# A two-layer diffusion backbone: the order of weight sums, block loads and drains in the Strassen part of layer 0's MLP

## The reference, cut to what matters

```
def _sq_relu_mlp(h, w1, w2):          # h: (768 tokens, 1024), w1: (1024, 4096), w2: (4096, 1024)
    return jnp.square(jax.nn.relu(h @ w1)) @ w2
...
x = _layernorm(DN_ALPHA * x + g2 * _sq_relu_mlp(x * (1.0 + s2) + sh2, ffn_w1[i], ffn_w2[i]), ln2_g[i], ln2_b[i])
```

## Time and profile before

| | us |
|---|---|
| median of 3 runs (lowest, highest) | 1959.92 (1959.57, 1962.16) |
| the profiled execution | 1959.92 |
| its span, first to last instruction | 1958.1 |
| PE busy | 1945.9 (99%) |
| DVE, ACT, POOL busy | 1312.5 (67%), 642.7 (33%), 385.9 (20%) |

### The profile page before, as it was taken

One profiled execution on the slowest core, in us unless ns is written; L12 is line 12 of the kernel. 1 busy time (PEld: TensorE's weight loads), 2 busy tenths in 40 slices (PEclk: granted clock), 3 DMA queues, 4 the chain that ended last, 5 costly groups with the idle time before them and its releaser, 6 DMA issues.

```text
span 1958.1 us, 25025 instructions
## 1 busy us (share of the span) xinstructions
PE 1945.9 (99%) x9525; PEld 1668.2 (85%) x9525; DVE 1312.5 (67%) x1892; ACT 642.7 (33%) x894; POOL 385.9 (20%) x360
## 2 busy tenths in 40 slices
PE   9999999999999999999999999999999999999998
PEld 6889889889889988899888888888888888888887
DVE  4756678688778776777865553644554477777778
ACT  3423222234323322232533223313323344344443
POOL 0300311322222222112350110020020026100004
PEclk9999999999999999999999999999999999999999
DMA  9623334335898998898322132121222125976656
GB/s 338 249 65 76 108 123 130 94 118 151 203 249 209 217 230 221 238 231 206 114 70 65 54 102 65 54 92 54 75 65 81 58 83 173 241 217 188 181 142 149
DMA packets 110833, 282.95 MB, mean 144 GB/s; under 512 B 16256, under 2 KB 29184, under 8 KB 110592
## 3 DMA queue, kind: packets, MB, share of 16 engines
q1 hardware_dynamic: 84496, 219.34, 33.8%
q0 software_dynamic: 24400, 58.21, 17.0%
q10 hardware_dynamic: 1824, 3.85, 0.6%
HBM read 234.67 MB, written 2.12 MB: 121 GB/s over the span
## 4 chain that ended last, share of the span: by engine, by line
PE 92%; DVE 2%; POOL 2%; DMA 2%; issue 2%; ACT 1%; SPq 0%; POOLq 0%; DVEq 0%; ACTq 0%
PE bank L999 17%; PE bank L1001 17%; PE bank L1000 17%; PE bank L1038 7%; PE bank L1039 7%; PE bank L1037 7%; PE bank L1400 3%; PE bank L1402 3%; PE bank L1403 3%; PE bank L1604 2%; PE bank L1602 2%; PE bank L1605 2%; PE bank L1307 1%; PE bank L1356 1%; PE bank L1219 1%
## 5 line engine op out<-in xcount | busy, mean ns | idle before, releaser
L2099 DVE TENSOR_TENSOR w_lo<-raw,w_hi 128x1024 fp32r<-128x1024 f32 x132 | 171.4, 1298 | 244.5 <-ACT w_hi L1628 244.4
L1628 ACT ACTIVATE w_hi<-raw 128x1024 fp32r<-128x1024 f32 x132 | 139.4, 1056 | 371.4 <-PE bank L1039 198.6
L1037 PE MATMUL bank<-w_hi,hT_hi 128*128 128x512 f32 x592 | 230.8, 390 | 0.0
L1038 PE MATMUL bank<-w_lo,hT_hi 128*128 128x512 f32 x592 | 230.5, 389 | 0.0
L1039 PE MATMUL bank<-w_hi,hT_lo 128*128 128x512 f32 x592 | 230.5, 389 | 0.0
L999 PE MATMUL bank<-w_hi,act_hi 128*128 128x512 f32 x504 | 198.4, 394 | 0.0
L1001 PE MATMUL bank<-w_hi,act_lo 128*128 128x512 f32 x504 | 196.6, 390 | 0.0
L1000 PE MATMUL bank<-w_lo,act_hi 128*128 128x512 f32 x504 | 196.5, 390 | 0.0
L999 PE MATMUL bank<-hT_hi,w_hi 128*128 128x384 f32 (+2 forms) x544 | 192.4, 354 | 0.0
L1001 PE MATMUL bank<-hT_hi,w_lo 128*128 128x384 f32 (+2 forms) x544 | 191.0, 351 | 0.0
L1000 PE MATMUL bank<-hT_lo,w_hi 128*128 128x384 f32 (+2 forms) x544 | 191.0, 351 | 0.0
(11 more groups left out here) (390 smaller groups left out, 4337.0 us busy)
## 6 DMA issues: line engine op xcount, KB each, us to landing
raw<-w_units_d SPq DMA_DIRECT2D x242, 512.0 KB, 3.8
mod<-mod_units_d SPq DMA_DIRECT2D x64, 384.0 KB, 4.4
wsum<-w_units_d SPq DMA_DIRECT2D x45, 512.0 KB, 4.5
wsum<-w_units_d POOLq DMA_DIRECT2D x26, 512.0 KB, 7.7
wsum<-wsum POOLq DMA_DIRECT2D x19, 512.0 KB, 6.7
bv<-mod_units_d SPq DMA_DIRECT2D x16, 512.0 KB, 3.6
mod<-mod_units_d SPq DMA_DIRECT2D x14, 512.0 KB, 7.9
res_lat<-rbuf POOLq DMA_DIRECT2D x28, 256.0 KB, 5.1
```

The costliest lines, as they stand in the source:

```text
L1037: nc.tensor.matmul(bank[t][:, :], hT_hi[:, kc, tt], hi[:, c], start=kc == 0, stop=False)
L1038: nc.tensor.matmul(bank[t][:, :], hT_hi[:, kc, tt], lo[:, c], start=False, stop=False)
L1628: nc.scalar.activation(halves_of(phase, k, i)[0], raw[:, s, :], ACT.Copy).then_inc(hi_done, 1)
L2099: tt(lo, raw[:, s, :], f32(hi), ALU.subtract).then_inc(lo_done, 1)
```

## The change

It moves T4's first term, its slot, and the order of several items. No arithmetic is added or removed except the source of T4's two terms. In the steady pieces:

- T4 is built in slot 1 (T1's): SP loads B21 into it a second time after T1's low half is made, and POOL adds T2's slot onto it. `raw`'s B21 is no longer read by POOL. This is one more load of 512 KB in each of seven pieces.
- SP loads the next piece's T1 base after T4's low half (before: after T1's), and T2's base once T4's sum has landed (before: after T4's low half). The load of the fourth down unit no longer waits for T4's sum.
- POOL's order of sums for the next piece is T3, T1, T2 (before: T1, T3, T2).
- DVE drains all of `down1` before it makes the low half of the next piece's T2 block (before: the last drain came behind it).

Around piece -1:

- SP loads B22 first and then waits for `shifted0` and loads T3's base (before: T3's base first).
- POOL issues T3's sum ahead of both halves of the adds (before: between them).
- ACT makes the high half of S2 (operand 3) ahead of down unit 6's.
- DVE makes S2's low half ahead of unit 6's, then does the first sum for S4 (L2872), and only then the six drains of `down0`. The low half of S4 (operand 4) moves from before the drains of `down1` to behind all six, and the low half of T2's block comes behind that.

```
-        SLOT0 = {T1: 1, T2: 2, T3: 0, T4: 2}
+        SLOT0 = {T1: 1, T2: 2, T3: 0, T4: 1}
...
+            sp.wait_ge(lo_done, before("splits", "ffn0a") + 7)
+            load_block0(0, B22, 2)
             sp.wait_ge(shifted0, 16 * TILES0)
             load_base0(0, T3)
-            sp.wait_ge(lo_done, before("splits", "ffn0a") + 7)
-            load_block0(0, B22, 2)
...
-                if more:
-                    done(2)
-                    load_base0(p + 1, T1)
+                done(2)
+                load_base0(p, T4)
...
                 done(5)
-                sp.wait_ge(t_sum0[T4], 16 * (p + 1))
                 load(at + 7, 3)
+                if more:
+                    sp.wait_ge(t_sum0[T4], 16 * (p + 1))
+                    load_base0(p + 1, T2)
                 done(6)
                 if more:
-                    load_base0(p + 1, T2)
+                    load_base0(p + 1, T1)
...
+                    operand0_hi(3, x22, s2_hi[:, :, :])
                     split_hi(phase, i, 6, used_unit(phase, i, 4))
-                    operand0_hi(3, x22, s2_hi[:, :, :])
...
-                    for t in range(2, TILES0 - 1):
+                    for t in range(2, TILES0):
                         drain0(p, 1, t)
-                        products(5, t - 2)
+                        if t < TILES0 - 1:
+                            products(5, t - 2)
                     block0_lo(p + 1, 1)
-                    drain0(p, 1, TILES0 - 1)
...
+                    operand0_lo(3, x22, s2_lo[:, :, :], s2_hi[:, :, :])
                     split_lo(phase, i, 6)
+
+                    tt(x22[:, :, :], x22[:, :, :], f32(hT_hi[:, second, t_first]), ALU.add).then_inc(x_whole, 1)
                     for t in range(TILES0):
                         drain0(-1, 0, t)
-                    operand0_lo(3, x22, s2_lo[:, :, :], s2_hi[:, :, :])
                     split_lo(phase, i, 7)
-
-                    tt(x22[:, :, :], x22[:, :, :], f32(hT_hi[:, second, t_first]), ALU.add).then_inc(x_whole, 1)
                     dve.wait_ge(x_whole, 4)
                     tt(x22[:, :, :], x22[:, :, :], f32(hT_lo[:, second, t_first]), ALU.add).then_inc(s_sum0, 1)
+                    block0_lo(0, 0)
+                    for t in range(TILES0):
+                        drain0(-1, 1, t)
                     dve.wait_ge(shifted0, 16 * TILES0)
                     operand0_lo(4, x22, s4_lo[:, :, :], s4_hi[:, :, :])
-                    block0_lo(0, 0)
-                    for t in range(TILES0 - 1):
-                        drain0(-1, 1, t)
                     block0_lo(0, 1)
-                    drain0(-1, 1, TILES0 - 1)
...
+                pool.wait_ge(t_base0[x], 16 * (p + 1))
+                if x == T2:
+                    pool.wait_ge(t_sum0[T1], 16 * (p + 1))
+                if x == T4:
+                    pool.wait_ge(t_sum0[T2], 16 * (p + 1))
                 out = wsum0[:, SLOT0[x], :]
-                if x == T4:
...
-                    other = raw[:, s, :]
+                if x in (T1, T3):
+                    out, other = two(out), up_block(p, B22 if x == T3 else B12)
                 else:
...
+                    other = wsum0[:, SLOT0[T1 if x == T2 else T2], :]
                 nc.gpsimd.dma_start(out, other, accum_op=ALU.add).then_inc(t_sum0[x], 16)
...
             shift_by_dma0()
+            weight_sum0(0, T3)
             pool.wait_ge(shifted0, 16 * TILES0)
             add0(-1, 0)
-            weight_sum0(0, T3)
             add0(-1, 1)
             for p in range(PIECES_F - 1):
                 weight_sum0(p, T4)
                 if p < PIECES_F - 2:
-                    for x in (T1, T3, T2):
+                    for x in (T3, T1, T2):
```

More of the change, by code:

```diff
@@ L3098, in weight_sum0 @@
             def weight_sum0(p, x):
-                out = wsum0[:, SLOT0[x], :]
-                if x == T4:
[L3103 to L3106, removed]
-                    other = raw[:, s, :]
-                else:
[L3109 to L3114, removed]
+                pool.wait_ge(t_base0[x], 16 * (p + 1))
[3 more added lines that the diff above has]
+                    pool.wait_ge(t_sum0[T2], 16 * (p + 1))
+                out = wsum0[:, SLOT0[x], :]
+                if x in (T1, T3):
+                    out, other = two(out), up_block(p, B22 if x == T3 else B12)
+                else:
+                    other = wsum0[:, SLOT0[T1 if x == T2 else T2], :]
                 nc.gpsimd.dma_start(out, other, accum_op=ALU.add).then_inc(t_sum0[x], 16)
```

## The result

The changed kernel takes 1971.65 us, the median of 6 runs (1969.70 to 1972.61), against 1960.17 for the kernel before (6 runs, 1959.31 to 1962.16). The ratio is 1.0056, with a 95% interval of 1.0044 to 1.0069: slower, by 11.5 us, where 5.7 were forecast. The time is 0.65 us above the top of the range.

A forecast was written before the change was run, and what follows sets the result against it. PE was taken as the bound, idle only 12.2 us, leaving almost nothing to win. Waits of 1.9 at down1.0 and 5.2 at q6, less the old 1.35, gave 5.7 us: 1959.9 + 5.7 = 1965.6, range 1960.2 to 1971.

The forecast's parts named there:

- Step 1, T3's base: Piece -1, SP: T3's base, now behind B22, is issued at 505.9 and lands 5.0 us later, at 510.9.
- Step 2, the sum: Piece -1, POOL: T3's sum waits for its base, issues at 511.25, takes 8.0 us and lands at 519.3.
- Step 3, POOL issues only so far ahead: Half 0's adds queue behind the sum: tile 5's goes out 5.5 us after the sum's landing and takes 5.1 us.
- Step 4, DVE's chain to q6: A down1 drain, S4's low half and T2's low half follow tile 5's add by 3.6 us; q6 starts at 533.5.
- SP's list is blocked then: While half 0's adds run, SP's modulation loads wait for S4's low half, so tile 5's add takes 5.1 us, not 6.3.
- Step 5, the loss at q5: q5 starts at 537.7 instead of 531.98, a 5.7 us loss: 1.9 at down1.0, 5.2 at q6, less the old 1.35.
- The steady pieces I cost at nothing: After piece -1: T4's later base and the new sum and drain orders have cover, so they add no time.
- The cover of 1.3 us: Piece 1, q4: PE stalls only if T4 is more than 1.3 us later than ACT wants it.
- T4's 2.7: Piece 0, where T4 is tightest: up to 2.7 us more if its base or sum takes its worst time.
- No real loss: Rival: the sum lands by 514.1, tile 5's adds finish before PE wants q6; 1960.5, no change; chance 0.15.
- T4 late: Rival: T4 late in most pieces, 0.7 us in each of seven, 4.9 us besides the 5.7: 1970.5; chance 0.14.
- gain: Rival: the old 1.35 us wait at q5 goes and nothing new comes, 1958.6, still no change; chance 0.05.

The follow-up runs named there:

- the start alone: The kernel before with only the change's reordering around piece -1, on SP, POOL, ACT and DVE: 1968.15 us, ratio 1.0046.
- The experiment with q3's low half: The kernel before, with DVE making the low half for q3 (B22) 1 to 5 times over in pieces 1 to 5: 1976.98 us, ratio 1.009.
- The steady part alone: The kernel before with only the change's edits to the steady pieces (T4's source and slot, orders of loads, sums and drains): 1963.62 us, ratio 1.0016.
- T4's base earlier: The kernel before with only the change's steady-piece edits, and SP issuing T4's base ahead of the modulation loads: 1962.97 us, ratio 1.0018.
- the last variant with T4's base earlier: The kernel before with the change's steady-piece edits, T4's base ahead of the modulation loads except in the last piece: 1961.49 us, ratio 1.0010.

## Why the prediction was wrong, step by step

**The profile read as the bound.** Right: the kernel before had almost nothing to win. Of nine other orders tried none is faster than it; two can't be told from it.

**Step 1, T3's base.** Issued at 506.41, forecast 505.9 (0.4 of it is the offset of that execution). Landed after 5.1 us, taken as 5.0. Undoing this step alone takes the loss from 11.5 to 4.5 us, and undoing the sum's new place alone takes it to 6.5. So the cause, shown, is the late base together with the sum ahead of the adds; either one without the other leaves q6 in time.

**Step 2, the sum.** 7.4 us, taken as 8.0: it landed at 519.5, against 519.3. The estimate of 3.2 us by the fit of the Trainium skill (DMA: Bandwidth & Descriptors, anatomy of one GpSimd DMA) stays too low. The list of issues in the changed kernel's profile has a median of 7.3 us for the 26 sums from memory (KB each, us to landing), and this one took 7.4:

```profile
wsum<-w_units_d POOLq DMA_DIRECT2D x26, 512.0 KB, 7.3
```

The landing by 514.1 that the prediction named for no loss isn't reached with the base behind B22. With the base first it is: the sum lands at 510.4 there, and q6 isn't late.

**Step 3, POOL issues only so far ahead.** Shown. Tile 5's add went out 5.4 us after the sum's landing (forecast 5.5) and landed after 5.1.

**Step 4, DVE's chain to q6.** q6 at 534.0, or 533.6 without the offset of 0.4: forecast 533.5. The experiment with DVE's old order shows that the order in this chain isn't what to blame: without it the adds that have SP's loads beside them land later, and q6 starts at nearly the same time. The argument "SP's list is blocked then" had the right fact, and its other side is that, as far as this one experiment tells, the blocking protected the adds.

**Step 5, the loss at q5.** Forecast 5.7, of which 1.9 at `down1.0` (measured 2.0), 5.2 at q6 (3.4, and 1.7 hidden in slow matmuls ahead of it) and -1.35. The mechanism and its size are right. But one step failed here: the price of a wait. The prediction priced a wait of 5 us as 5 us. It is followed by half clock, which costs 1.5 us in the changed kernel and 2.4 in the one with the start alone. The experiment with q3's low half shows that this needs nothing of the change: half clock came after both long waits there too.

**"The steady pieces I cost at nothing": the other step that failed.** The changed kernel loses 1.4 us there in its profile, and 1.0 us in the LayerNorm behind. The steady part alone loses 4.2 us by its median. The cover of 1.3 us against ACT was worked out for piece 1 with a base of 5.6 us and a sum of 5.9. The sums of the changed kernel after 540 us took 4.6 to 9.1 us, with a median of 6.7. In piece 4 the sum landed at 807.57, after 7.4 us, 1.9 us after ACT wanted it, and PE waited 0.6 us for T4's low half. The prediction wrote down these waits, but as a rival to the main case with a chance of 0.14 and as the very top of its range. They don't exclude the loss at q6. They come on top of it. The range's top has a slip as well: a base of 7.6, a sum of 9.5 and a t5 that is 1.2 late add 2.6 + 1.5 + 1.2 = 5.3 us to 1965.6, which is 1970.9 already. The "part of T4's 2.7" that the sentence counts in has no room in it.

**The rivals.** No real loss is excluded. T4 late was true in two or three pieces, not most, together with the forecast case. No gain came: where the old wait of 1.35 us at q5 went, another was there, of 1.1 us at q6 with the sum first and of 1.4 us at q3 with the sum between the adds and a late base.

**The sum of the parts.** 8.7 and 4.2 us make 12.9, and the changed kernel loses 11.5. The profiles show where the two overlap, by the starts of the matmuls: T4 is late in piece 0 with the steady part alone (1.4 us at q4's first matmul, 1.6 in all) and not in the changed kernel, where PE comes to q4 7.6 us later; and the slow clock after q6 costs 2.4 us with the start alone and 1.5 in the changed kernel. That PE's lateness is what gave T4 its time in piece 0 is argued, not tested.

**What stays open.** Of the 11.5 us between the medians the profiles explain 10.1. The profiled execution was one of the quicker ones (1970.03; the median of the others is 1971.65), and I don't know what the others lose and where. The loss in the LayerNorm is in the profiles of the changed kernel (1.0 us), the steady part (1.2), T3's base first (2.1) and T4's base earlier (0.9). It is not in those of the last variant with T4's base earlier, of the sum between the adds and of DVE's old order, which hold the same steady part, or the same but for the place of one load. So it doesn't follow from the order of the lists alone, and it may come and go between executions of one kernel. No run shows that, or its cause. And the wait of 1.8 us at `down1.0` has a clock of 0.69 behind it in the changed kernel, and full clock in the three others that have the same wait (the start alone, T3's base first, the sum between the adds). Why isn't settled.

## What to carry to other kernels

When a DMA is put ahead of others in a queue that issues only so far ahead, ask how late its own input may come. With the base early, the sum ahead of the adds cost nothing that can be told, in the kernel before. With the rest of the change in place, the loss was 4.5 us with the base early and the sum first, 6.5 with the base late and the sum between the adds, and 11.5 with the base late and the sum first. Price a wait of PE by what follows it too, and count each thin cover as a term of its own with some expected loss, added to the main case; kept as rivals of each other, they made the range too narrow.

## What the hardware showed that was not expected

- A wait of PE can cost more than itself. After 0.8 us the granted clock stayed at 2.4 GHz; after 3.2 to 6.4 us it was at 1.2 GHz, in all five waits of that length, for about 3 us or more, at a cost of 1.5 to 3.0 us. Near 2 us both were seen: 2.1 us at q3 had full clock behind it, 2.15 us at q7 half clock for about 3 us, and 1.8 us at `down1.0` had 0.69 behind it in one kernel of four.
- With loads of SP beside them (the kernel with ACT's and DVE's old order), the adds of tiles 1 to 3 took 9.0 to 10.1 us, against 3.4 to 5.5 in the changed kernel, and POOL issued nothing for 6.6 us.
- A 384 KB modulation load with a 512 KB load ahead of it in SP's queue took 7.6 us from issue to landing, where the same load took 5.4 in the kernel before. The median of all 64 such loads was 6.0 us in that kernel and 4.4 in the kernel before, where the longest took 10.0.
